# GpSimd alternates the two expert tables' gathers, the V rows one group behind the U rows

## The reference

```
q = (h @ w_peer_q).reshape(B, S, 8, 2, 128)
s = einsum('bshcd,hcnd->bshcn', q, peer_sub_keys)         # 2 x 128 scores per head
top_s, top_i = top_k(s, 16)                               # then the best 16 of the 256 sums
expert_idx, g = ..., softmax(best_s)
a = gelu(einsum('td,ted->te', h, peer_u[expert_idx]))     # one dot per expert
out = einsum('te,ted->td', g * a, peer_v[expert_idx])     # weighted sum of rows
```

## Time and profile before

| | |
|---|---|
| runs | 1005.27 us median of 3, 998.52 to 1005.81 |
| the profiled execution | 1007.17 us, its span 1005.4 us |
| granted TensorE clock, mean | 0.900 |
| PE busy | 796.7 us (79%) |
| DVE busy | 605.9 us (60%) |
| POOL busy | 491.5 us (49%) |
| ACT busy | 192.4 us (19%) |
| indirect gathers | 268.47 MB, 70.9% of the 16 DMA engines' span |
| chain that ended last | POOL 36%, PE 29%, issue 18%, DVE 7% |

### The profile page before, as it was taken

How to read it: one execution, slowest core, us unless ns; L and a number is a source line. 1 busy time by engine, 2 the same in 40 slices (tenths; PEclk the granted TensorE clock), 3 DMA queues, 4 the chain that set the end, 5 groups by cost and what they waited for, 6 DMA issues and landing times.

```text
span 1005.4 us, 8411 instructions
## 1 busy us (share of the span) xinstructions
PE 796.7 (79%) x2726; PEld 463.6 (46%) x2726; DVE 605.9 (60%) x1359; ACT 192.4 (19%) x483; POOL 491.5 (49%) x529
## 2 busy tenths in 40 slices
PE   5999999999694769777696969696676859595764
PEld 5877588867352435334342524243333425252321
DVE  6245675236777575747557474848474665778455
ACT  1012122201313121213022112212120312212111
POOL 1000000000767566756666666666566666666662
PEclk9999999999797979988887979797988879797988
DMA  9998956582999999999999999999999999999994
GB/s 350 375 365 317 343 188 247 196 265 84 341 359 380 328 373 376 376 353 372 347 367 353 366 370 360 376 363 368 365 373 345 358 361 362 368 365 396 358 410 152
DMA packets 112282, 338.48 MB, mean 337 GB/s; under 512 B 9184, under 2 KB 20976, under 8 KB 112112
## 3 DMA queue, kind: packets, MB, share of 16 engines
q0 software_dynamic: 73728, 268.47, 70.9%
q1 hardware_dynamic: 35936, 67.11, 18.7%
q10 hardware_dynamic: 2576, 2.37, 0.8%
HBM read 336.87 MB, written 1.05 MB: 336 GB/s over the span
## 4 chain that ended last, share of the span: by engine, by line
POOL 36%; PE 29%; issue 18%; DVE 7%; another core or an unknown queue 6%; DMA 3%; ACT 1%; POOLq 0%; DVEq 0%; ACTq 0%
POOL ring L351 36%; PE bank L987 10%; PE bank L1159 6%; DVE ring L832 3%; PE bank L1090 3%; PE bank L980 3%; DMA ring<-in_peer_u_dram,small 1%; PE bank L1104 1%; PE h_ps L936 1%; PE bank L1123 1%; PE h_ps L953 1%; PE h_ps L941 1%; DMA ring<-in_peer_v_dram,small 1%; DMA x_sb<-in_x_dram 0%
## 5 line engine op out<-in xcount | busy, mean ns | idle before, releaser
L832 DVE CUSTOM_DVE_ANT_0 ring<-ring,h_ps 128x1024 f32<-128x1024 f32 x256 | 310.9, 1221 | 225.0 <-DMA ring<-in_peer_u_dram,small 203.4
L351 POOL DMA_INDIRECT ring<-in_peer_u_dram,small x256 | 247.5, 967 | 283.7 <-DVE small L813 203.5
L1159 PE MATMUL bank<-ring,small 128*128 128x512 f32 x512 | 258.4, 669 | 150.9 <-ACT small L519 87.2
L351 POOL DMA_INDIRECT ring<-in_peer_v_dram,small x256 | 240.0, 938 | 170.3 <-remote 89.0
L1159 PEld LDWEIGHTS bank<-ring,small 128*128 128x128 f32 x512 | 109.3, 217 | 290.5 <-issue 290.5
L1159 PE MATMUL bank<-ring,h_sb 128*128 128x512 f32 x500 | 225.1, 608 | 16.4 <-ACT h_sb L519 6.5
L1159 PEld LDWEIGHTS bank<-ring,h_sb 128*128 128x128 f32 x500 | 96.5, 196 | 135.5 <-issue 128.5
L987 PE MATMUL bank<-hT,ring 128*128 128x256 f32 x448 | 102.3, 389 | 1.1 <-ACT hT L402 1.1
L987 PEld LDWEIGHTS bank<-hT,ring 128*128 128x128 f32 x448 | 86.3, 194 | 16.3 <-issue 4.4
L1123 PE MATMUL bank<-hT,wpq 128*128 128x128 f32 x512 | 67.9, 288 | 17.6 <-issue 17.1
L1123 PEld LDWEIGHTS bank<-hT,wpq 128*128 128x128 f32 x512 | 65.1, 202 | 27.0 <-issue 26.4
(11 more groups left out here) (159 smaller groups left out, 515.8 us busy)
## 6 DMA issues: line engine op xcount, KB each, us to landing
ring<-in_w_cond_dram SPq DMA_DIRECT2D x10, 2048.0 KB, 13.8
ring<-in_w_in_dram SPq DMA_DIRECT2D x8, 2048.0 KB, 12.3
wpq<-in_w_peer_q_dram SPq DMA_DIRECT2D x8, 1024.0 KB, 12.0
ring<-in_w_cond_dram SPq DMA_DIRECT2D x4, 1024.0 KB, 14.5
ring<-in_w_out_dram SPq DMA_DIRECT2D x2, 2048.0 KB, 10.7
ring<-in_peer_u_dram,small POOLq DMA_INDIRECT x256
ring<-in_peer_v_dram,small POOLq DMA_INDIRECT x256
ring<-in_w_in_dram SPq DMA_DIRECT2D x2, 1024.0 KB, 13.5
```

The source lines that it names most:

```text
L351: nc.gpsimd.indirect_dma_start(out=dst[e], out_offset=None, in_=table[0], in_offset=bass.IndirectOffsetOnAxis(ap=idx[:, k:k + 1], axis=0)) ...
L832: V.tensor_tensor_reduce(u_ring[e], u_ring[e], h_ps[:], 1.0, 0.0, ALU.mult, ALU.add, acol[:, g, e:e + 1]).then_inc(dots_done, 1)
L1159: last = T.matmul(bank[ACC_BANKS[t][m]][:], diag_of(p, g)[:, e, :], v_ring[e][:, m * BLK:(m + 1) * BLK], start=False, stop=end, skip_group ...
```

## The change

POOL issues a U row of group n and a V row of group n - 1 in turn, over 33 rounds; the first round has only U rows and the last only V rows. The U wait is no longer for all dots of the group before, but ahead of every second U row for the two slots concerned. The V wait has the same form as before. `idx` gets a third buffer, as V rows now read a pair's indices while the next pairs' are written; DVE's wait ahead of the write follows that. `score(p + 2)` moves from the start of `add_rows(p + 1)` to the place ahead of row 6 of the second group in `add_rows(p)`; `score(1)` stays at the start of `add_rows(0)`. The lists `V_SLOT`, `V_TURN` and `V_BEFORE` give for V row j = 8n + e its slot, turn and predecessor; with eight rows they give the values that were there before. No arithmetic and no byte moved is added or removed.

```diff
--- before.py
+++ after.py
@@ -64,6 +64,10 @@
 GT1, SH2, SC2, GT2 = range(4)
 LN_G, LN_B = 0, 1
 UROW, VROW, ROWS = 4, 12, 16
+V_ROWS = 2 * PAIRS * GROUP
+V_SLOT = [j % GROUP for j in range(V_ROWS)]
+V_TURN = [j // GROUP for j in range(V_ROWS)]
+V_BEFORE = [j - GROUP for j in range(V_ROWS)]
 
 
 
@@ -154,7 +158,7 @@
         acol = small[:, 2822:2838].rearrange("p (a k) -> p a k", a=2)
         gcol = small[:, 2838:2854].rearrange("p (a k) -> p a k", a=2)
         wts = small[:, 2854:2870].rearrange("p (a k) -> p a k", a=2)
-        idx = small[:, 2870:2902].bitcast(U32)
+        idx = small[:, 2870:2918].bitcast(U32)
 
         def row(first, e):
             r = (first + e) % ROWS
@@ -343,31 +347,39 @@
             nc.gpsimd.affine_select(out=spat_nat, in_=spat_nat, compare_op=ALU.is_ge, fill=0.0, base=0,
                                     pattern=[[0, HEADS], [-1, P]], channel_multiplier=1).then_inc(spat_masked, 1)
 
-            def gather_pair(i, a):
-
-                p = 2 * i + a
-
-                def gather(table, dst, e, k, landed):
-                    nc.gpsimd.indirect_dma_start(
-                        out=dst[e], out_offset=None, in_=table[0],
-                        in_offset=bass.IndirectOffsetOnAxis(ap=idx[:, k:k + 1], axis=0)).then_inc(landed[e], 16)
-
-                pool.wait_ge(idx_ready, p + 1)
-                for g in range(2):
-                    n = 2 * p + g
-                    first = a * TOPK + g * GROUP
-
-                    pool.wait_ge(dots_done, GROUP * n + GROUP)
-                    for e in range(GROUP):
-                        gather(peer_u, u_ring, e, first + e, u_in)
-                    for e in range(GROUP):
-                        if e % 2 == 0:
-                            pool.wait_ge(v_used, GROUP * n + e + 2)
-                        gather(peer_v, v_ring, e, first + e, v_in)
-
-            for i in range(0, PAIRS // 2):
-                gather_pair(i, 0)
-                gather_pair(i, 1)
+            def gather(table, dst, n, e, landed):
+
+                p = n // 2
+                k = p % 3 * TOPK + n % 2 * GROUP + e
+                nc.gpsimd.indirect_dma_start(
+                    out=dst, out_offset=None, in_=table[0],
+                    in_offset=bass.IndirectOffsetOnAxis(ap=idx[:, k:k + 1], axis=0)).then_inc(landed, 16)
+
+            def u_row(n, e):
+
+                if e == 0 and n % 2 == 0:
+                    pool.wait_ge(idx_ready, n // 2 + 1)
+                if n == 0:
+                    if e == 0:
+                        pool.wait_ge(dots_done, GROUP)
+                elif e % 2 == 0:
+                    pool.wait_ge(dots_done, GROUP * n + e + 2)
+                gather(peer_u, u_ring[e], n, e, u_in[e])
+
+            def v_row(n, e):
+
+                j = GROUP * n + e
+                if e % 2 == 0:
+                    before = max(V_BEFORE[j], V_BEFORE[j + 1])
+                    pool.wait_ge(v_used, GROUP + max(before + 1, 0))
+                gather(peer_v, v_ring[V_SLOT[j]], n, e, v_in[V_SLOT[j]])
+
+            for n in range(2 * PAIRS + 1):
+                for e in range(GROUP):
+                    if n < 2 * PAIRS:
+                        u_row(n, e)
+                    if n:
+                        v_row(n - 1, e)
 
 
         @block.scalar
@@ -807,10 +819,10 @@
                                      .broadcast_to([P, 2, TOPK, TOPK]), ALU.mult))
                 step(V.tensor_reduce(sel, oh, AX_X, ALU.add))
                 assert step.n == TOPK_STEPS, step.n
-                if not (isinstance(p, int) and p == 0):
-
-                    dve.wait_ge(v_used, p * TOPK - TOPK + GROUP)
-                V.scalar_tensor_tensor(out=idx[:, a * TOPK:(a + 1) * TOPK], in0=sel[:, 0:TOPK], scalar=float(NKEYS),
+                if p >= 3:
+
+                    dve.wait_ge(v_used, GROUP + (p - 2) * TOPK)
+                V.scalar_tensor_tensor(out=idx[:, p % 3 * TOPK:(p % 3 + 1) * TOPK], in0=sel[:, 0:TOPK], scalar=float(NKEYS),
                                        in1=sel[:, TOPK:2 * TOPK], op0=ALU.mult, op1=ALU.add).then_inc(idx_ready, 1)
 
             def weights(p, a, g):
@@ -859,11 +871,12 @@
                 dve.wait_ge(wts_ready, n + 1)
                 dve.wait_ge(dots_done, GROUP * (n + 2))
                 for e in DVE_ROWS:
-                    dve.wait_ge(v_in[e], 16 * (n + 1))
+                    j = GROUP * n + e
+                    dve.wait_ge(v_in[V_SLOT[j]], 16 * (V_TURN[j] + 1))
                     if e == DVE_ROWS[0]:
-                        link(V.tensor_scalar(base, v_ring[e], wts[:, 1, e:e + 1], None, ALU.mult))
+                        link(V.tensor_scalar(base, v_ring[V_SLOT[j]], wts[:, 1, e:e + 1], None, ALU.mult))
                     else:
-                        link(V.scalar_tensor_tensor(out=base, in0=v_ring[e], scalar=wts[:, 1, e:e + 1], in1=base,
+                        link(V.scalar_tensor_tensor(out=base, in0=v_ring[V_SLOT[j]], scalar=wts[:, 1, e:e + 1], in1=base,
                                                     op0=ALU.mult, op1=ALU.add))
                 link(V.tensor_tensor(base, base, cond[:, GT2, :], ALU.mult))
                 link(V.scalar_tensor_tensor(out=base, in0=x_sb[:, t, :], scalar=ALPHA, in1=base, op0=ALU.mult, op1=ALU.add))
@@ -1146,17 +1159,20 @@
             def add_rows(p):
 
                 t = p // HEADS
-                if p + 1 < PAIRS:
-                    score(p + 1)
+                if p == 0:
+                    score(1)
                 for g in range(2):
                     n = 2 * p + g
                     rows = PE_ROWS if n == 2 * PAIRS - 1 else range(GROUP)
                     for i, e in enumerate(rows):
-                        pe.wait_ge(v_in[e], 16 * (n + 1))
+                        if (g, e) == (1, GROUP - 2) and p + 2 < PAIRS:
+                            score(p + 2)
+                        j = GROUP * n + e
+                        pe.wait_ge(v_in[V_SLOT[j]], 16 * (V_TURN[j] + 1))
                         pe.wait_ge(diag_ready, GROUP * n + i + 1)
                         end = p % HEADS == HEADS - 1 and (g, i) == (1, len(rows) - 1)
                         for m in range(2):
-                            last = T.matmul(bank[ACC_BANKS[t][m]][:], diag_of(p, g)[:, e, :], v_ring[e][:, m * BLK:(m + 1) * BLK],
+                            last = T.matmul(bank[ACC_BANKS[t][m]][:], diag_of(p, g)[:, e, :], v_ring[V_SLOT[j]][:, m * BLK:(m + 1) * BLK],
                                             start=False, stop=end, skip_group_check=True)
                             if end and p == PAIRS - 1:
                                 last.then_inc(acc_ready, 1)
```

## The result

The changed kernel takes 1030.74 us (median of 4 runs, 1023.83 to 1043.25), the kernel before 1004.92 us (4 runs): ratio 1.0248, 95% interval 1.0176 to 1.0320. It is slower, and the forecast of 990 us had the sign wrong.

What follows compares the result with a forecast made beforehand. POOL's gather issue was taken as the bound, with V-row waits on top. From 1007.2 us, -25 for the waits, +5 and +3 at the ends gave 990 us; the 8-in-10 range was 938 to 1045.

Steps and rivals of the forecast that it cites:

- What bounds the kernel: POOL in the expert part: issuing 512 gathers takes 636 us, with 99.9 us of waits ahead of V rows on top.
- The U wait: POOL ahead of U rows: two dots needed, rows issued 14 issues back; gain 0, bounds 0 and 3 us.
- The V wait: POOL ahead of V rows: slack goes from 5.9 to 7.9 us; late counts still cost 2 to 3 us a pair.
- The scores: DVE before `topk_halves` and the chain behind it: 5 us of POOL waits a pair, 75 against 99.9, gain 25.
- The third index buffer: DVE's new wait before writing indices lies 32 rows back: cost 0.
- the ends: First and last rounds: 5 us lost after `norm_and_modulate(1)`, 3 us at `finish(0)`, 0 at the very end.
- The scores' chain is the new bound, slower: DVE before `topk_halves`, weights and indices behind it: 8 to 9 us of POOL waiting a pair, 1043 us; chance 0.25.
- PE's increments: PE's counts: the skill's 26 ns spacing would make none late, but the trace showed them taking 4 to 8 us.

Runs made afterwards that it cites:

- Score at row 3: Changed kernel with score(p + 2) ahead of row 3 of the second group instead of row 6: 1017.63 us, 1.0059.
- pausing POOL: Changed kernel, score(p + 2) at second group's row 3, query(p + 2) at first group's row 4, POOL waiting for indices before second group's U row 4: 1057.88 us.
- waiting for four back: Changed kernel, with POOL waiting ahead of each gather until the one issued four before it has landed: 1093.93 us, 1.0790.
- score at row 0: Changed kernel with score(p + 2) ahead of row 0 of the second group instead of row 6: 1059.95 us.
- root(6) first: Changed kernel, score(p + 2) at second group's row 3, query(p + 2) at first group's row 4, ACT taking root(6) ahead of save_q(15): 1040.97 us.

## Why the prediction was wrong, by its own steps

**What bounds the kernel.** Right in that it is not the transfers: with half the bytes the time is the same. That issue is the bound, with the pauses on top, describes where POOL's time goes; what sets the pauses' sum is open, as said above. The 358 GB/s at which the Trainium skill (DMA: Bandwidth & Descriptors, Where 436 GB/s comes from) puts reads from HBM is no bound here either: the kernel before ran at 366 GB/s, and at 184 GB/s it was no faster.

**The U wait.** Right for the kernel before (0.9973). In the changed kernel this wait became the place where all of DVE's lateness reaches POOL, 59.0 us; "it gives room for a late DVE" counted 14 issues of room, and the late DVE used it up. The step had put this at nothing.

**The V wait.** Near: from 99.9 to 74.7 us; the marks were 50 to 80.

**The scores: the step that failed.** The step put 75 us on POOL's waits; they are 120.4 beyond the gaps. Two of its terms failed. The first is the length of `topk_sums`, taken at the 5.5 us of the one pair read in the earlier trace rows. That pair, like nearly all of the kernel before, began right after POOL's pause. Moved out of it, the same instructions take 8.07 us in the mean and 13.4 in the pair shown, so there the indices came 33 us after the issue of V row 5 at 779.80 and not 25 to 29. The second was left out: behind the indices U row 0 still needs two dots of the second group, which DVE takes after `topk_sums`. In the pair shown they are done at 815.1, 2.3 us after the indices, and in each of the 14 pairs whose scores the change moves U row 0 was issued 3.0 to 6.9 us after the indices. Over these 14 pairs the indices came at +23.9 to +34.8, +28.9 in the mean, and U row 0 went out at +33.3 in the mean, where the forecast needed it at +26. Score at row 3, pausing POOL and waiting for four back show how far the length goes with POOL: it is 5.3 to 5.6 us in 13 of 15 pairs, 6.1 in the mean, and 5.5 in the mean.

The wait ahead of it came out in size: 3.9 us a pair (58.6 over 15; 4 to 8 were forecast), and the scores' copy at +15.7 in the pair shown, where 15.6 to 19.6 had been worked out. But that was in part luck. The forecast had PE done with V row 5 at +8.5 to +11 and the count 4 to 8 us late. In eight of the 14 pairs, the one shown among them, the scores' count was at ACT within 0.1 us, and in the other six it was 3.5 to 14 us late. In the pair shown PE itself was late. It was done with V row 5 at 795.0, +15.2, after pauses between its matmuls that the profile puts down to nothing, and its clock was granted at 0.56 from 790 to 795 us:

```profile
784.57 0.59 PE L1175 MATMUL bank<-ring,h_sb 128*128 128x512 f32 x1 [0.82 <-issue]
786.67 0.59 PE L1175 MATMUL bank<-ring,h_sb 128*128 128x512 f32 x1 [1.51 <-issue]
788.77 1.01 PE L1175 MATMUL bank<-ring,h_sb 128*128 128x512 f32 x1 [1.51 <-issue]
```

**The third index buffer, the ends.** 0 as said. After `norm_and_modulate(1)` POOL lost 3.1 us, not 5. After finish(0) 9.05 us, not 3: ACT takes root(6) behind save_q(15), which waits for a late count, so DVE stood 14.42 us:

```profile
930.83 0.38 ACT L501 ACTIVATE small<-bank 128x256 f32<-128x256 f32 x1 [15.65 <-remote]
...
932.52 0.29 ACT L396 ACTIVATE std<-moments,eps 128x1 f32<-128x1 f32 x1
932.92 0.16 DVE L757 RECIPROCAL std<-std 128x1 f32<-128x1 f32 x1 [14.42 <-ACT std L396]
...
937.08 0.94 POOL L354 DMA_INDIRECT ring<-in_peer_u_dram,small  x1 [9.05 <-DVE small L844]
```

**The rivals.** "The scores' chain is the new bound, slower" was right in sign and size, and its place is the chain where the time went: it asked for 8.5 us a pair, 1043 us; it was 133.7 / 15 = 8.9, and 1030.74 and 1043.65. Of its three signs one came: POOL's waits were over 130 us, but DVE waited 3.9 us a pair for the scores and not 8, and the granted clock was 0.89 and not under 0.85. So its number was in part luck, as it had neither the longer `topk_sums` nor the two dots. Its condition, that counts come only when POOL pauses, was in the rows and was given 0.25; it is too strong, since eight of 14 score counts were prompt. I had named the sign of it and then priced the step as if only PE's counts were late.

**PE's increments.** The Trainium skill (TensorE: Matmul & The Clock Gate, The cost: per-tile semaphore tail) has increments 26 ns apart. The trace shows counts as prompt where POOL is slowed (q copied 0.04 us after `query`) and not where it issues back to back (15 us). Counts that had been held up then stand 0.05 to 0.06 us apart, about twice that figure; the measured one holds here.

**What stays open.** Shown is that the counts of PE and DVE are late, that this needs POOL's gathers beside them, and that it goes neither by bytes nor by indices. By what path a gather holds up a count isn't shown, nor whether it is the issuing or the number of rows under way. How the loss divides between the wait ahead of `topk_halves`, the longer `topk_sums` and the two dots isn't settled: with half the bytes `topk_sums` took only 6.68 us in the mean, the wait was 111.2 us, and the loss was the same 2.5%. What is shown is that the place of the scores decides, as score at row 3 alone gave most of it back. Why PE paused between matmuls in the pair shown is open. The 0.6% that score at row 3 still loses are not settled; its two late `topk_sums`, of 12.5 and 13.2 us, are candidates.

## What to carry to other kernels

Where GpSimd issues indirect gathers back to back, as here, count every chain of short dependent steps as slow unless it falls right behind a pause of GpSimd, and move it there before anything else. A step's length read from one place of the trace holds only for that phase: read it in all its instances and against what GpSimd does meanwhile. Halving the bytes of each transfer tells in one run whether bandwidth bounds the kernel, whatever the DMA share says.

## What the hardware did that I had not expected

- A DMA share of 0.97 at 366 GB/s was no bound: with half the bytes it was 0.64 at 184 GB/s and the time the same.
- An indirect gather costs POOL 0.94 us for 128 indices and 0.90 for 64, and two memsets fit into the 0.30 us between two of them for nothing.
- The count of DVE's own last instruction reached DVE up to 6.8 us late while POOL issued (score at row 0, and root(6) first). With the wait for four back no step of `topk_sums` waited over 0.05 us for it.
- Gathers came 1.43 to 1.45 us apart over the steady middle of every version that DVE didn't hold up, at 128 or 64 indices and 4 or 2 KB a row, though POOL can issue one in 1.24. Whether this is a pace of the gathers isn't shown, as the other engines' work was the same too.
